# The meta tile of the attention's weighted latent sums as split products

## The reference, cut to what matters

```
s = jnp.einsum('bqhc,bqkc->bqhk', q_lat, kv_sel) * (ATT_HEAD_DIM ** -0.5)
p = jax.nn.softmax(jnp.where(valid[:, :, None, :], s, -jnp.inf), axis=-1)
o_lat = jnp.einsum('bqhk,bqkc->bqhc', p, kv_sel)
y_att = jnp.einsum('bthc,hcd->bthd', o_lat, w_uv)
```

## Time and profile before

| | |
|---|---|
| median of 3 runs | 1018.18 us (1017.34 to 1019.1) |
| the profiled execution | 1017.49 us |
| its span, first to last instruction | 1015.8 us |
| TensorE's granted clock, mean | 0.998 |
| busy: PE, DVE, ACT, POOL | 996.9, 714.0, 493.8, 118.1 us |

### The profile page before, as it was taken

How to read it: one execution, slowest core, us unless ns; L and a number is a source line. 1 busy time by engine, 2 the same in 40 slices (tenths; PEclk the granted TensorE clock), 3 DMA queues, 4 the chain that set the end, 5 groups by cost and what they waited for, 6 DMA issues and landing times.

```text
span 1015.8 us, 18999 instructions
## 1 busy us (share of the span) xinstructions
PE 996.9 (98%) x7028; PEld 907.9 (89%) x7028; DVE 714.0 (70%) x1317; ACT 493.8 (49%) x868; POOL 118.1 (12%) x92
## 2 busy tenths in 40 slices
PE   9999999999999999999999999999999999999996
PEld 8999999999999988699765668889999999988886
DVE  6988888887322264699997523699989889942236
ACT  6656665566121264546346522576656665812121
POOL 0000000001121262045302205320000000000000
PEclk9999999999999999999999999999999999999999
DMA  7233332323223313132110102113323232333212
GB/s 252 84 100 107 102 105 90 116 80 105 86 86 111 113 44 116 36 123 82 44 42 1 43 1 83 43 42 126 124 83 124 85 121 96 125 103 101 98 57 84
DMA packets 30849, 90.48 MB, mean 89 GB/s; under 512 B 4689, under 2 KB 5329, under 8 KB 30801
## 3 DMA queue, kind: packets, MB, share of 16 engines
q1 hardware_dynamic: 30800, 89.83, 26.7%
HBM read 87.72 MB, written 2.10 MB: 88 GB/s over the span
## 4 chain that ended last, share of the span: by engine, by line
PE 81%; DVE 15%; ACT 2%; issue 1%; DMA 0%; SPq 0%; DVEq 0%; ACTq 0%
PE ps L1229 38%; PE ps L1287 22%; PE ps L1152 9%; DVE sc L2201 3%; DVE top L2200 3%; PE ps L1714 2%; PE ps L1424 1%; PE ps L1692 1%; DVE qk L2240 1%; PE ps L1705 1%; DVE wlo L1877 1%; PE ps L1489 1%; PE ps L1722 1%; PE ps L1337 1%; PE ps L1335 1%
## 5 line engine op out<-in xcount | busy, mean ns | idle before, releaser
L1229 PE MATMUL ps<-tsum,whi 128*128 128x264 f32 (+1 forms) x1280 | 243.1, 282 | 0.5 <-ACT ht L790 0.5
L1229 PEld LDWEIGHTS ps<-tsum,whi 128*128 128x128 f32 x1280 | 202.3, 188 | 0.7 <-issue 0.7
L1229 PE MATMUL ps<-tsum,wlo 128*128 128x264 f32 (+1 forms) x640 | 180.3, 282 | 0.0
L1229 PE MATMUL ps<-xh,whi 128*128 128x264 f32 (+1 forms) x480 | 135.4, 282 | 0.3 <-ACT sil L790 0.3
L1229 PE MATMUL ps<-xl,whi 128*128 128x264 f32 (+1 forms) x480 | 135.5, 282 | 0.0
L1229 PE MATMUL ps<-xh,wlo 128*128 128x264 f32 (+1 forms) x480 | 135.3, 282 | 0.0
L729 ACT ACTIVATE whi<-wraw 128x1408 fp32r<-128x1408 f32 (+1 forms) x48 | 74.6, 1555 | 123.0 <-PE ps L1287 123.0
L1787 DVE TENSOR_TENSOR wlo<-wraw,whi 128x1408 fp32r<-128x1408 f32 (+1 forms) x38 | 70.0, 1843 | 85.3 <-ACT whi L729 85.3
L1287 PE MATMUL ps<-hh,whi 128*128 128x264 f32 (+1 forms) x462 | 124.2, 323 | 0.0
L1287 PE MATMUL ps<-hh,wlo 128*128 128x264 f32 (+1 forms) x462 | 123.5, 322 | 0.0
L1287 PE MATMUL ps<-hl,whi 128*128 128x264 f32 (+1 forms) x462 | 123.4, 321 | 0.0
(11 more groups left out here) (287 smaller groups left out, 1828.0 us busy)
## 6 DMA issues: line engine op xcount, KB each, us to landing
wraw<-in_ffn_w_gate SPq DMA_DIRECT2D x43, 512.0 KB, 4.2
wraw<-in_ffn_w_up SPq DMA_DIRECT2D x42, 512.0 KB, 4.3
wraw<-in_ffn_w_down SPq DMA_DIRECT2D x32, 384.0 KB, 3.2
wraw<-in_ffn_w_down SPq DMA_DIRECT2D x32, 320.0 KB, 3.5
wraw<-in_w_in SPq DMA_DIRECT2D x19, 512.0 KB, 4.5
wraw<-in_w_out SPq DMA_DIRECT2D x8, 512.0 KB, 4.4
out<-zrow SPq DMA_DIRECT2D x8, 256.0 KB, 2.0
x<-in_x SPq DMA_DIRECT2D x3, 528.0 KB, 7.5
```

The lines of the kernel that those rows point to most:

```text
L1229: mm = pe.matmul(ps[:, bank, 0:(HT, HALF_SEQ)[p // 2]], w[:, k * P:(k + 1) * P], v[:, k, :], start=(first and k == 0 and n == 0), stop=(k ...
```

## The change

For the meta tile alone, the product of latents and turned weights is made from split parts. The latents of the 16 meta tokens are split once (on ScalarE and, in `split_latents`, on GpSimd) into a high part `chi` and a low part `clo`, and the high part is written twice, 32 partitions apart, into a zeroed tile `meta_c` of 64 partitions. The turned meta weights (32 rows now, of which 16 count) are rounded by ScalarE into partitions 0 to 31 of `pt_h`; VectorE subtracts that from the PSUM bank and writes the low part into partitions 32 to 63. Then two float32r products are made: the low latents by the high weights (16 partitions), and `meta_c` by both parts at once (64 partitions). All other tiles are copied and multiplied as before. ScalarE copies all meta tiles and the odd others, VectorE subtracts at all meta tiles and copies the even others. The high and other tiles have buffers of their own now, and two of the four score buffers moved.

```diff
@@ split_latents, GpSimd, called between mix_lo(9) and causal_mask(3) @@
+pool.wait_ge(c_hi, 1)
+pool.wait_ge(ct_turned, 1)
+m = N_META
+pool.tensor_tensor(clo[0:m, 0, :], cmat[0:m, 0, :], chi[0:m, 0, :].bitcast(F32), ALU.subtract).then_inc(c_lo, 1)
+link(pool.memset(meta_c[:, :].bitcast(F32), 0.0))
+for e, r in enumerate((0, 32)):
+    pool.wait_ge(c_lo, e + 1)
+    pool.tensor_copy(meta_c[r:r + m, :], chi[0:m, 0, :].bitcast(F32)).then_inc(c_lo, 1)
+pool.wait_ge(c_lo, 3)
@@ mixer, ScalarE, between the copies of ct and hi(MIX0 + 4, 0, UW, False) @@
+act.activation(chi[0:N_META, 0, :], cmat[0:N_META, 0, :], ACT.Copy).then_inc(c_hi, 1)
@@ copy_odd, ScalarE @@
-if t % 2 == 1:
-    ...
-    act.activation(pt_flat[0:ROWS[i], 512:1024], ps[0:ROWS[i], 1, :], ACT.Copy)\
-        .then_inc(pt_odd, 1)
+if i and t % 2 == 0:
+    continue
+act.wait_ge(pt_turned, t + 1)
+if t >= 2:
+    act.wait_ge(pv_step, t - 1)
+dst, src = (pt[t % 2], ps[:, t % 2, :]) if i else (pt_h[t % 2][0:META_ROWS, :], ps[0:META_ROWS, t % 2, :])
+act.activation(dst, src, ACT.Copy).then_inc(pt_hi, 1)
@@ copy_even, VectorE @@
+if i == 0:
+    dve.wait_ge(pt_hi, copies_by_act(t))
+    ins = dve.tensor_tensor(pt_h[t % 2][32:32 + META_ROWS, :], ps[0:META_ROWS, t % 2, :],
+                            pt_h[t % 2][0:META_ROWS, :].bitcast(F32), ALU.subtract)
+elif t % 2 == 0:
     ...
+    ins = dve.tensor_copy(pt[t % 2], ps[:, t % 2, :])
@@ weigh, TensorE @@
+if i == 0:
+    pe.wait_ge(pt_hi, copies_by_act(t))
+    if G >= 1:
+        pe.wait_ge(ol_ready, G)
+    pe.wait_ge(c_lo, 3)
+    m = N_META
+    pe.matmul(ps[:, 3, :], clo[0:m, 0, :], pt_h[t % 2][0:m, :], start=True, stop=False)
+    copied_weights(t)
+    pe.matmul(ps[:, 3, :], meta_c[:, :], pt_h[t % 2][0:64, :], start=False, stop=False).then_inc(pv_step, 1)
+    return
+copied_weights(t)
+pe.matmul(ps[:, 3, :], cmat[:, i, :], pt[t % 2], start=False, stop=(i == 1 + G // 2)).then_inc(pv_step, 1)
@@ buffers @@
-sbuf = [sil[:, 0, :], sil[:, 1, :], pt_flat[:, 1024:1024 + T], pt_flat[:, 1024 + T:1024 + 2 * T]]
+sbuf = [sil[:, 0, :], sil[:, 1, :], pt_flat[:, 2048:2048 + T], qk[:, 3, :]]
```

More of the change, by code:

```diff
@@ L98 @@
 DROPS = END[1] - TOPK
+META_ROWS = 32
 def build(nc, a, out):
@@ L179, in build @@
             ct = sb("ct", [P, T], F32, s)
-            cs = sb("cs", [P, NT, 256], F32, s)
+            with ExitStack() as c_scope:
+                cs = sb("cs", [P, NT, 256], F32, c_scope)
+            c_parts = sb("c_parts", [P, NT, 256], F32R, s)
+            clo, chi = c_parts[:, :, 0:LAT], c_parts[:, :, LAT:2 * LAT]
             wuk = sb("wuk", [P, 4, LAT], F32, s)
@@ L184, in build @@
             upad = sb("upad", [P, 4 * (T + CONV - 1)], F32, s)
-            v1 = sb("v1", [P, NT, ML_H, VW], F32, s)
+            with ExitStack() as v_scope:
+                v1 = sb("v1", [P, NT, ML_H, VW], F32, v_scope)
+            pts = sb("pts", [P, NT * ML_H * VW], F32R, s)
+            meta_c = sb("meta_c", [64, LAT], F32R, s)
             sg = sb("sg", [P, 4, T], F32, s)
@@ L283, in build, with meta_turn, copies_by_act, copies_by_dve @@
         pt_flat = v1[:, :, :, :].rearrange("p j h v -> p (j h v)")
-        sbuf = [sil[:, 0, :], sil[:, 1, :], pt_flat[:, 1024:1024 + T], pt_flat[:, 1024 + T:1024 + 2 * T]]
+        sbuf = [sil[:, 0, :], sil[:, 1, :], pt_flat[:, 2048:2048 + T], qk[:, 3, :]]
+        pt_h = [pts[:, e * 512:(e + 1) * 512] for e in range(2)]
+        pt = [pt_flat[:, (2 + e) * 512:(3 + e) * 512] for e in range(2)]
+        def meta_turn(t):
+            return t in TP0
+        def copies_by_act(t):
+            return sum(meta_turn(v) or v % 2 == 1 for v in range(t + 1))
+        def copies_by_dve(t):
+            return sum(meta_turn(v) or v % 2 == 0 for v in range(t + 1))
         qk_flat = qk[:, :, :].rearrange("p c t -> p (c t)")
@@ L398, in build @@
         pt_turned = sem("pt_turned")
-        pt_even = sem("pt_even")
-        pt_odd = sem("pt_odd")
+        pt_hi = sem("pt_hi")
+        pt_lo = sem("pt_lo")
+        c_hi = sem("c_hi")
+        c_lo = sem("c_lo")
         pv_step = sem("pv_step")
@@ L674, in decay_mask, with split_latents @@
                                        pattern=[[0, 4], [1, P]], channel_multiplier=-1).then_inc(wt_masked, 1)
+                def split_latents():
+                    pool.wait_ge(c_hi, 1)
[7 more added lines that the diff above has]
+                    pool.wait_ge(c_lo, 3)
                 pool.wait_ge(idx_masked, NT - 1)
@@ L694, in mixer @@
                 mix_lo(9)
+                split_latents()
                 causal_mask(3)
@@ L1694, in scores, with copied_weights @@
                     mm.then_inc(s_done, 1)
+                def copied_weights(t):
+                    if t % 2 == 1 and not meta_turn(t):
+                        pe.wait_ge(pt_hi, copies_by_act(t))
+                    else:
+                        pe.wait_ge(pt_lo, copies_by_dve(t))
                 def turn(G, i):
@@ L1702, in turn @@
                     if t >= 2:
-                        pe.wait_ge(pt_even if t % 2 == 0 else pt_odd, t // 2)
+                        copied_weights(t - 2)
                     for q in range(4):
-                        mm = pe.transpose(ps[0:ROWS[i], t % 2, q * P:(q + 1) * P], pbuf[G % 2][:, q, START[i]:END[i]],
-                                          ident[:, :])
+                        k0, k1 = (START[i], END[i]) if i else (0, META_ROWS)
+                        mm = pe.transpose(ps[0:k1 - k0, t % 2, q * P:(q + 1) * P], pbuf[G % 2][:, q, k0:k1], ident[:, :])
                     mm.then_inc(pt_turned, 1)
@@ L2365, in copy_even @@
                         t = TP0[G] + i
-                        if t % 2 == 0:
+                        if i == 0:
[3 more added lines that the diff above has]
+                        elif t % 2 == 0:
                             dve.wait_ge(pt_turned, t + 1)
@@ L2369, in copy_even @@
                                 dve.wait_ge(pv_step, t - 1)
-                            dve.tensor_copy(pt_flat[0:ROWS[i], 0:512], ps[0:ROWS[i], 0, :]).then_inc(pt_even, 1)
+                            ins = dve.tensor_copy(pt[t % 2], ps[:, t % 2, :])
+                        else:
+                            continue
+                        ins.then_inc(pt_lo, 1)
                 def late_round(G, place):
```

3 lines of the change are left out of this document (removed).

## The result

The changed kernel takes 1024.16 us (median of 4 runs, 1023.35 to 1025.46), the kernel before beside it 1017.8 (4 runs, 1017.34 to 1019.1; the forecast had started from 1018.18, the median of three of them): a ratio of 1.0062 [1.0044, 1.0079], so 6.3 us slower. The profiled executions differ by the same: 1023.35 against 1017.49, spans 1021.6 and 1015.8.

A forecast was written before the change was run, and what follows sets the result against it. Bound: the loop masked, exponential, copy, product across VectorE, ScalarE and TensorE in passes 4 and 5, TensorE in 6 and 7. Attention 3.5 plus 0.2 ahead gives 3.7: 1021.2 profiled, 1021.9 as median; range 1018.9 to 1024.6 us.

The forecast's parts named there:

- the collision: Rival, pass 2: GpSimd's mLSTM subtraction blocks VectorE's norm work, making VectorE and `project` 1.2 us later; 1023.1 us, chance 0.21.
- ahead of the attention: Before the attention, ScalarE's small extra rounding delays a weight rounding VectorE waits for: 0.2 us, bounds 0 and 0.6.
- up to `project` (passes 1, 2): VectorE's waits for ScalarE's rounding delay the copy of the sums, so `project` starts 1.23 us late.
- the rest of pass 3: Subtraction 0.4 us later than the old copy, but only the last tile's product needs what follows: 0.
- pass 4: VectorE waits for ScalarE's rounding, copies t = 8 1.95 us late; arrives in full, since TensorE already waited.
- pass 5: Behind `normalise`, the subtraction comes 0.41 us later than the old copy; a product waiting for VectorE is 0.41 late.
- pass 6: Subtraction 1.46 us late, partly absorbed by VectorE's 0.73 idle before the copy of t = 16: 0.37 late.
- pass 7: The second product may start before TensorE gets there, so the cheaper product's gain stands: 0.51 us won.
- pass 8: The meta subtraction stands behind the output's, so the turn after the second product starts 0.05 us later.
- The stalls: VectorE stands idle mid-pass until ScalarE's rounding: 1.25 us in pass 2, about 1.2 in pass 1, 1.3 in pass 4.
- The pair of products: Two float32r meta products on TensorE take 0.54 us instead of 1.05, needing 0.51 less in each of eight passes.
- The held instruction: VectorE's instruction behind each subtraction might be held, some 0.08 us in each of six passes, 0.5 in all; left out.

The follow-up runs named there:

- the kernel with one product: Changed kernel with copies, waits and subtraction kept, but one float32 product over 16 partitions replacing both float32r products, low parts left out: 1026.88 us.
- tuned, all rows: Changed kernel with the subtraction moved to where it need not wait and both meta products over 128 zero-filled partitions, behind the waits: 1020.33 us.
- the kernel with the low part elsewhere: Changed kernel with VectorE's subtraction writing to a spare tile from partition 0 in six of eight passes, which use an old low part: 1024.52 us.

## Why the prediction was right, and where it was short

The direction, the main mechanism and the range held: 3.7 forecast, 6.3 measured. But 1024.16 lies above the forecast's own range (1020.6 to 1023.1; the bounds it names for its terms make it 1020.8 to 1023.2) and above the 1023.1 of the collision; only the wide range of 1018.9 to 1024.6 holds it. Every step inside the attention came out higher than forecast. By its own steps, in us, the lateness of each stretch against before:

| step | forecast | measured |
|---|---|---|
| ahead of the attention | +0.2 | -0.20 |
| up to `project` (passes 1, 2) | +1.23 | +2.66 |
| the rest of pass 3 | 0 | +0.24 |
| pass 4 | +1.95 | +2.06 |
| pass 5 | +0.41 | +0.53 |
| pass 6 | +0.37 | +0.41 |
| pass 7 | -0.51 | -0.19 |
| pass 8 | +0.05 | +0.35 |
| sum | 3.7 | 5.86 |

*The stalls* were sized well. Pass 4 was read from two rows, the start of ScalarE's rounding and an idle time that was already there; VectorE's wait came out at 1.26 for some 1.3, TensorE's at 2.98 for about 3. Passes 5 and 6 are 0.12 and 0.04 off. Without the subtraction they all vanish.

*The rest of pass 3* was put at 0 and came out at 0.24: the product of its last tile, which ran without a wait before, stood 0.28 for VectorE's copy.

*The collision* is the largest term that was missing. It stood among the rivals with a chance of 0.21, priced at 1.2; it happened, at 1.1, on top of the forecast. The offsets had been worked out and all agreed (GpSimd about 1.6 after ScalarE's rounding, in the middle of the norm work); I held against it that the norm work reads one SBUF tensor, while the only row of a collision read two. That was a reason to doubt the size, and not enough to leave the term at nothing: the offsets said it would happen. With its 1.1 and 0.23 more in pass 1, the stretch up to `project` is explained to 0.1.

On this the Trainium skill, page "SBUF — State Buffer", section "SBUF: two separate sides", names a second case beside two SBUF inputs: a VectorE operation in a two-port mode. The 2.19 against 1.12 of the norm work, which reads one SBUF tensor and two per-partition scalars, speaks for that case; which mode it runs in, no row shows.

*The pair of products* was taken at 0.54, from products of 128 partitions among their like. At 16 and 64 partitions it is 0.85. The 0.3 is seen whole in pass 7 (-0.19 for -0.51) and for 0.2 in pass 8; elsewhere it lies beside waits. The rows named the cause beforehand, had they been read against each other: the product over 16 partitions took 1.05 to its successor, and a product over 128 was never timed that way, only by its busy length, which was the same (1.12 and 1.13). In pass 7 of the same trace one takes 0.86 to its successor:

```profile
588.21 1.02 PE L1714 MATMUL ps<-v,cs 128*128 128x512 f32 x2
589.07 0.60 PE L1705 MATMUL ps<-ident,qi 128*128 128x128 f32 x4
```

*The held instruction* was weighed and left out. The price is 0.10 to 0.12 a piece (0.08 had been estimated). In pass 8 it is seen twice, since the subtraction is held behind its neighbour too: two pitches (start to start) of 0.72 and 0.71 in VectorE's timeline, where the kernel before has 0.61 (594.03 to 594.64).

```profile
599.54 0.69 DVE L2408 TENSOR_TENSOR xl<-ps,xh 128x512 fp32r<-128x512 f32 x1 [2.34 <-ACT xh L1162]
600.26 0.68 DVE L2418 TENSOR_TENSOR pts<-ps,pts 32x512 fp32r<-32x512 f32 x1
600.97 0.69 DVE L2424 COPY v<-ps 128x512 f32<-128x512 f32 x1
```

These pitches agree with the Trainium skill, page "VectorE: DVE Perf Modes", section "Two Vector instructions with no wait between them", by which an instruction whose output starts in another group of 32 partitions than the last one is held.

*The step ahead of the attention* was right where it can be read, and its total was luck. ScalarE's weight rounding starts 0.36 after the last copy of `ct` (425.62 to 425.98) and started 0.16 after it before (425.93 to 426.09): the small rounding costs the 0.20 forecast. But that copy came 0.31 earlier than in the kernel before, ahead of the first instruction that the change adds, and the attention's start varies from 528.88 to 530.81 over the kernels profiled. So 0.4 of the shortfall was hidden: from the attention's start on, the forecast was 3.5 and the lateness 6.06.

*Open*: the profiled execution of the changed kernel is the fastest of its four runs, and kept its clock at 1.00 in the attention. Others lie up to 2.1 above it. In other kernels with gaps of this kind the clock fell in some executions; whether that is the rest of the changed kernel's spread was not seen in a trace of it.

## What to carry to other kernels

A cheaper product on the busiest engine is worth only what its new helpers leave: before counting it, walk each helper to its place in its engine's list, see what then stands behind its wait, and look for a place where that engine has other work to put in front (here 10.87 became 9.54). When an edit shifts a list by half a microsecond, check what GpSimd does at the new offset, and give a collision whose offsets all agree a term of its own in the sum; here it was worth 1.1 of the 2.4 us that were missing. Small products among large ones may gain more from zero rows up to the neighbours' height than from a cheaper type: that change alone made the kernel before 1.7 us faster.

## What the hardware showed that was not expected

A product of 512 columns between products of 128 partitions takes longer when it spans fewer: float32 1.05 us over 16 partitions and 0.86 over 128, float32r 0.42 over 64 and 0.24 over 128 to the next turn. In the timeline of the stationary loads the changed kernel's stand between the products, each with idle time in front, and 0.18 long:

```profile
592.37 0.18 PEld L1760 LDWEIGHTS ps<-pts,c_parts 16*128 16x128 f32 x1 [0.34 <-issue]
592.80 0.18 PEld L1762 LDWEIGHTS ps<-pts,meta_c 64*128 64x128 f32 x1 [0.25 <-issue]
593.22 0.42 PEld L1749 LDWEIGHTS ps<-ident,qi 128*128 128x128 f32 x4 [0.24 <-issue]
```

The 0.19 by which a pitch of 0.42 exceeds 0.23 is about the length of such a load. That the load isn't done ahead is the reading that fits; the runs show the cost and what removes it, not the inside of it. The kernel without the subtraction fits in part. There the load for 32 partitions starts at 585.53, 0.11 behind that for 16 and under its product, and the pitch of 0.34 is near the 0.31 of a pair of equal height; the turn's load, for 128, starts at 586.08 with 0.37 of idle time ahead of it. But its pitch is 0.32 and not 0.42, and why 32 partitions cost less than 64 stays open.

TensorE's granted clock after a gap is not the same from one execution to the next. In the kernel with one product TensorE stood 1.50 us up to 536.95 and worked without a gap from there; the granted clock was 1.00 (2.4 GHz) until 538.5, 0.50 (1.2 GHz) from 539 to 542 and 1.00 again behind it, which makes the 0.82 and 0.75 of the two windows above:

```profile
539.50:540.00 0.50, 0.50 (x4) 0.50 (x4) 0.00 (x0) 0.50 (x2) 0.39 (x1) 0.50 0.00 0
```

In "tuned, all rows", after the same 1.50 (up to 537.93), it stayed at 1.00:

```profile
536.00:540.00 4.00, 2.50 (x12) 1.66 (x12) 2.96 (x10) 3.20 (x12) 0.01 (x1) 1.00 0.00 0
```

The changed kernel stood 2.98 and kept 1.00; the kernel with the low part elsewhere stood 2.97, up to 564.61, and had 0.65 from 564 to 568 us. A price for such a fall can therefore be put on a gap only as a chance.
